# The last two experts' rows reach their frames through TensorE, and the work behind a mixture of experts is put in another order (two-layer encoder step, one core)

## What is computed

```python
def hier_moe(x, w_group, b_group, w_expert, b_expert, w1, w3, w2):
    xt = x.reshape(B * T, D)
    g_logits = xt @ w_group + b_group                 # 4 groups
    grp = argmax(g_logits);  p_grp = softmax(g_logits)[grp]
    e_logits = (xt @ w_expert + b_expert).reshape(-1, 4, 8)
    topv, topi = top_k(e_logits[grp], 2)              # 2 of the group's 8 experts
    gates = one_hot(grp) * (one_hot(topi) * softmax(topv)) * p_grp     # (T, 32)
    h = silu(xt @ w1[e]) * (xt @ w3[e]) * gates[e]    # per expert, width 256
    return sum_e(h @ w2[e])

for layer in (0, 1):
    h = h + mixer(rmsnorm(h, norm_mix[layer]))        # layer 1: short convolution
    h = h + hier_moe(rmsnorm(h, norm_ffn[layer]), ...)
```

## Time and profile before

| | |
|---|---|
| median of 3 runs | 1164.1 us |
| the profiled execution | 1163.0 us, span 1161.3 us |
| TensorE busy | 1012.0 us (87%) |
| VectorE, ScalarE, GpSimd busy | 390.5, 307.0, 189.6 us |
| mean granted TensorE clock | 0.941 |
| bytes moved | 282.80 MB, mean 244 GB/s |
| mixture of layer 0 / of layer 1, router to last scatter | about 360 to 637 / 870 to 1139 us |

### The profile page before, as it was taken

The page is one execution under the profiler, slowest core; times in us unless marked ns, Lnnn a source line. Parts: engine busy times, 40 slices in busy tenths (PEclk is TensorE's granted clock), DMA queues, the critical chain, the costliest instruction groups (busy, mean ns, idle before and its releaser), DMA issues.

```text
span 1161.3 us, 20224 instructions
## 1 busy us (share of the span) xinstructions
PE 1012.0 (87%) x8611; PEld 788.6 (68%) x8611; DVE 390.5 (34%) x861; ACT 307.0 (26%) x714; POOL 189.6 (16%) x188
## 2 busy tenths in 40 slices
PE   6999999989999899777875499999998999778781
PEld 6999898965898655444442399999996655444440
DVE  5242464257337211101101755546355111011104
ACT  6255344256224121101102421221131121011110
POOL 7344213120000223112111000000001222121110
PEclk9999998989899999989888699999999999898896
DMA  6432121420736999999996724243667999999976
GB/s 224 96 98 91 38 75 60 112 93 2 249 158 239 361 416 415 417 416 416 416 410 191 214 56 109 55 109 145 183 163 291 396 415 418 416 417 416 416 287 241
DMA packets 115011, 282.80 MB, mean 244 GB/s; under 512 B 23102, under 2 KB 70250, under 8 KB 98504
## 3 DMA queue, kind: packets, MB, share of 16 engines
q1 hardware_dynamic: 105192, 263.64, 61.1%
q0 software_dynamic: 9728, 17.85, 4.1%
HBM read 270.55 MB, written 27.02 MB: 256 GB/s over the span
## 4 chain that ended last, share of the span: by engine, by line
PE 62%; SPq 15%; DMA 15%; DVE 5%; issue 2%; ACT 1%; POOL 0%; DVEq 0%; POOLq 0%; ACTq 0%
PE banks L1046 12%; DMA w<-in_w_dram 11%; SPq L397 10%; PE banks L913 10%; PE banks L681 10%; PE banks L974 9%; PE banks L680 6%; SPq L400 5%; PE banks L985 4%; DVE H L1790 1%; PE banks L652 1%; DMA yab<-y_rows 1%; PE banks L874 1%; PE banks L858 1%; PE banks L968 1%
## 5 line engine op out<-in xcount | busy, mean ns | idle before, releaser
L974 PE MATMUL banks<-w,xgT 128*64 128x256 f32 x2048 | 261.5, 416 | 65.7 <-DMA w<-in_w_dram 64.5
L974 PEld LDWEIGHTS banks<-w,xgT 128*64 128x64 f32 x2048 | 161.9, 150 | 172.9 <-DMA w<-in_w_dram 72.9
L1728 DVE TENSOR_TENSOR hh<-banks,sg 128x128 f32<-128x128 f32 x64 | 18.6, 291 | 407.1 <-ACT sg L1294 407.1
L590 POOL DMA_INDIRECT y_rows<-ys,yidx x64 | 63.6, 994 | 381.4 <-ACT ys L1302 380.0
L985 PE MATMUL banks<-w,hT 128*64 128x512 f32 x512 | 116.9, 599 | 0.0
L1046 PE MATMUL banks<-xc_hi,wc_hi 128*128 128x272 f32 x384 | 111.0, 289 | 2.1 <-DVE xc_lo L1368 2.1
L1046 PE MATMUL banks<-xc_hi,wc_lo 128*128 128x272 f32 x384 | 111.2, 289 | 0.0
L1046 PE MATMUL banks<-xc_lo,wc_hi 128*128 128x272 f32 x384 | 110.6, 288 | 0.0
L586 POOL DMA_INDIRECT xr<-x_rows,gidx x32 | 33.5, 1046 | 400.0 <-DVE yidx L1714 382.2
L576 POOL TENSOR_TENSOR wab_lo<-wab,wab_hi 128x512 fp32r<-128x512 f32 x56 | 77.0, 1406 | 129.6 <-ACT wab_hi L1106 128.7
L681 PE MATMUL banks<-wab_hi,xc_hi 128*128 128x256 f32 (+1 forms) x320 | 93.7, 293 | 4.0 <-DVE xp_lo L1368 2.2
(11 more groups left out here) (283 smaller groups left out, 1765.1 us busy)
## 6 DMA issues: line engine op xcount, KB each, us to landing
w<-in_w_dram SPq DMA_DIRECT2D x192, 1024.0 KB, 23.0
wab<-in_w_in_ab_dram SPq DMA_DIRECT2D x13, 1024.0 KB, 5.2
wc<-in_w_in_c_dram SPq DMA_DIRECT2D x24, 512.0 KB, 5.3
yab<-y_rows SPq DMA_DIRECT2D x16, 512.0 KB, 6.7
wo<-in_w_out_ab_dram SPq DMA_DIRECT2D x4, 1024.0 KB, 7.1
x_rows<-XF SPq DMA_DIRECT2D x8, 512.0 KB, 3.3
wo<-in_w_out_c_dram SPq DMA_DIRECT2D x4, 1024.0 KB, 5.5
H<-in_x_prompt_dram SPq DMA_DIRECT2D x4, 512.0 KB, 8.9
```

The source lines that it names most:

```text
L590: pool.indirect_dma_start(y_dram[l][:, :], bass.IndirectOffsetOnAxis(ap=index.bitcast(U32), axis=0), ys[i][:, :], None, bounds_check=4 * T ...
L974: last = pe.matmul(bank[hb][64 * f:64 * f + 64, 0:2 * P].rearrange("p (w j) -> p w j", w=2), xgT[i][:, k, 64 * ab:64 * ab + 64], w13[s][:, ...
```

## The change

Seven edits, all in the mixtures and at their end.

1. **Experts 30 and 31** are no longer scattered. GpSimd scatters rows of zeros in their place at the start of the mixture (`zs_out`), so that `y_rows` is whole without them. SyncE's return loads wait for 30 experts instead of 32, and for these zero rows.
2. VectorE works out place and share of each frame in the last pair (8 small operations in `route`, 10 of 128 x 128 for `toks`), TensorE transposes them (`last_pair_T`, 10 transpositions behind the first pair's `hidden`), ScalarE copies them out (3 copies, `tkT_ok`, for which the first `rows_out` waits).
3. **`last_pair_rows`**: for each chunk 4 matmuls (weights `toks_T`, 64 rows; moving `ys`, 512 columns) give the last pair's share of 1024 features in two banks, and `combine` is now one more addition from PSUM. The two old operations are called `returned`.
4. **Router**: the two streams of 8 matmuls are taken by turns, after all chunks are there; one signal instead of two.
5. **Order at the boundary**: VectorE splits conv block 0 (`wc_lo`) only behind chunk 3; TensorE begins the first half with the two terms that don't need it; ScalarE makes `wc_hi` of block 0 between the squares of chunks 1 and 2.
6. `yab` lies at other addresses (free during the experts). SyncE's loads for the next router wait for the last `last_pair_rows` (`cb_mm`), since `toks_T` lies there.
7. The last mixture combines chunks in the order 0, 1, 2, 4, 3. Three semaphores of the recurrence are merged into `exp_ok`.

```diff
+COMBINE_BANKS = [0, 2, 4, 2, 6]
...
-        yab = [at(f"yab{c}", (132, 140, MISC, MISC + 8, MISC + 16)[c], [P, 2, D]) for c in range(NC)]
+        yab = [at(f"yab{c}", (132, 152, 160, 144, 172)[c], [P, 2, D]) for c in range(NC)]
...
+        SCATTERS = [NE // 4 - (j >= 2) for j in range(4)]
...
-                sp.wait_ge(y_mm, NE * (l + 1))
+                sp.wait_ge(y_mm, NE * l + NE - 2)
                 sp.wait_ge(cnt_ok, l + 1)
                 for j in range(4):
-                    sp.wait_ge(scat[j], 16 * (NE // 4) * (l + 1))
+                    sp.wait_ge(scat[j], 16 * SCATTERS[j] * (l + 1))
+                sp.wait_ge(zs_out, 32 * (l + 1))
...
             sp.wait_ge(lg_mm, 2)
+            sp.wait_ge(cb_mm, NC)
             router_load(1)
...
                 for u_ in range(2):
                     fetch(u_, gidx[:, u_:u_ + 1], xr_in[u_])
+                tie(pool.memset(ys[3][:], 0.0))
+                pool.wait_ge(ix_ok, 2 * l + 2)
+                for e in (NE - 2, NE - 1):
+                    pool.indirect_dma_start(y_dram[l][:, :], ... ys[3][:, :] ...).then_inc(zs_out, 16)
...
-                    for e in (2 * u_, 2 * u_ + 1):
+                    for e in (2 * u_, 2 * u_ + 1)[0:2 * (u_ < PAIRS - 1)]:
...
-                for p0, t, chunks, done in ((0, slice(0, 2 * P), 2, lgh_mm), (64, slice(2 * P, T), NC, lg_mm)):
-                    pe.wait_ge(xt_a, NC * (2 * l + 1) + chunks)
-                    pe.wait_ge(xt_d, NC * (2 * l + 1) + chunks)
-                    for k in range(KT):
+                pe.wait_ge(xt_a, NC * (2 * l + 2))
+                pe.wait_ge(xt_d, NC * (2 * l + 2))
+                for k in range(KT):
+                    for p0, t in ((0, slice(0, 2 * P)), (64, slice(2 * P, T))):
                         last = pe.matmul(bank[0][p0:p0 + NR, 0:t.stop - t.start], wr[:, k, :], XT[l][:, k, t], ...)
...
+                    if u_ == 0:
+                        last_pair_T()
...
+                        if e == 0:
+                            pe.wait_ge(tkT_ok, l + 1)
                         rows_out(SLOTS[l][e % 6], ab, y_mm)
...
+            def last_pair_rows(l, c):
+                b = COMBINE_BANKS[c]
+                for ab in range(2):
+                    for n in range(2):
+                        half = slice(64 * n, 64 * n + 64)
+                        w = toks_T[c // 2][half, c % 2, ab, :] if c < 4 else toks_T4[half, ab, :]
+                        last = pe.matmul(bank[b + n][0:ROWS[c], :], w, ys[2 + ab][half, :], start=ab == 0, stop=ab == 1)
+                last.then_inc(cb_mm, 1)
             mixture(0)
+            for c in range(3):
+                last_pair_rows(0, c)
...
-            for c in range(3):
-                norm_transpose(2, c)
+            norm_transpose(2, 0)
+            norm_transpose(2, 1)
+            pe.wait_ge(h_ok, NC + 2)
+            last_pair_rows(0, 3)
+            norm_transpose(2, 2)
+            frames_ready(1)
+            last_pair_rows(0, 4)
+            pe.wait_ge(wc_hi_ok, 1)
+            frames_ready(3)
+            conv_terms(0, 0, 0, (0, 1))
+            conv_terms(0, 0, 1, (0, 1))
+            pe.wait_ge(h_ok, NC + 4)
+            conv_terms(0, 0, 2, (0, 1))
             pe.wait_ge(wc_lo_ok, 1)
-            frames_ready(3)
-            for a in range(3):
-                if a == 2:
-                    norm_transpose(2, 3)
-                    norm_transpose(2, 4)
-                conv_terms(0, 0, a)
+            for a in range(2):
+                conv_terms(0, 0, a, (2,))
+            norm_transpose(2, 3)
+            norm_transpose(2, 4)
+            conv_terms(0, 0, 2, (2,))
             frames_ready(NC)
...
+            square(2, 0)
+            square(2, 1)
             conv_hi(0)
+            square(2, 2)
+            mixer_in_hi(2, range(3))
             conv_hi(1)
-            for c in range(3):
-                square(2, c)
-            mixer_in_hi(2, range(3))
...
+                    returned(0, 0)
+                    returned(0, 1)
+                    combine(0, 0)
+                    returned(0, 2)
+                    combine(0, 1)
+                    norm(2, 0)
+                    combine(0, 2)
+                    norm(2, 1)
+                    norm(2, 2)
+                    mixer_in_lo(2, xc_lo, range(3))
+                    returned(0, 3)
+                    combine(0, 3)
                     conv_lo(0)
...
+                    returned(0, 4)
+                    combine(0, 4)
+                    norm(2, 3)
+                    norm(2, 4)
+                    mixer_in_lo(2, xc_lo, (3, 4))
...
+            def combine(l, c):
+                n, b = ROWS[c], COMBINE_BANKS[c]
+                done = c if l == 0 else (0, 1, 2, 4, 3)[c]
+                dve.wait_ge(cb_mm, NC * l + done + 1)
+                h = H[0:n, c, :].rearrange("p (a d) -> p a d", a=2)
+                tie(dve.tensor_tensor(h, banks[0:n, b:b + 2, :], h, ALU.add))
                 dve.nop().then_inc(h_ok, 1)
```

More of the change, by code:

```diff
@@ L516, in _ @@
             mixture(1)
[L517 to L518 removed]
+            for i, c in enumerate((0, 1, 2, 4, 3)):
+                sp.wait_ge(h_ok, 3 * NC + i + 1)
                 dst = y_prompt[0, c * P:(c + 1) * P, :] if c < 4 else y_sample[0, :, :]
@@ L1077, in _ @@
             mixture(1)
+            for c in range(3):
+                last_pair_rows(1, c)
+            pe.wait_ge(h_ok, 3 * NC + 1)
+            last_pair_rows(1, 4)
+            pe.wait_ge(h_ok, 3 * NC + 2)
+            last_pair_rows(1, 3)
         @block.scalar
@@ L1723, in mixture @@
                 xg_high(0).then_inc(xg_d, 1)
+                for c in range(NC):
+                    n = ROWS[c]
+                    for e in range(2):
+                        last = dve.tensor_scalar(toks[c][0:n, e, :], slot_no[0:n, :], place[0:n, c, e:e + 1], share[0:n, c, e:e + 1],
+                                                 ALU.is_equal, ALU.mult)
+                last.then_inc(rk_ok, 1)
                 for u_ in range(PAIRS):
```

96 lines of the change are left out of this document (62 added, 34 removed).

## The result

| | before | after |
|---|---|---|
| median | 1163.18 us (8 runs) | 1166.95 us (8 runs, 1165.43 to 1168.04) |
| ratio | | 1.0028, 95% interval 1.0015 to 1.0041 |
| profiled execution, span | 1163.0, 1161.3 us | 1168.04, 1166.3 us |
| TensorE, VectorE, ScalarE busy | 1012.0, 390.5, 307.0 us | 1029.6, 411.2, 308.9 us |
| mean granted clock | 0.941 | 0.947 |

The forecast was 1164.2, in 1157.2 to 1170.8. The ratio is the one on record, with its interval; the quotient of the two medians alone is 1.0032. The profiled execution of after was the longest of its eight, 1.1 us above the median; its span is 5.0 us longer than that of before.

A forecast was written before the change was run, and what follows sets the result against it. The prediction took weight streaming to bound the mixtures and a chain of waits the rest. Terms of -1.7, -0.7, +6.0 and -3.5 us sum to +0.1, giving 1163.1, plus 1.1 for the median: 1164.2 us, range 1157.2 to 1170.8.

The forecast's parts named there:

- What bounds the kernel: Whole kernel: weight streaming at 416 GB/s sets the mixtures; outside them the chain of waits, including layer 0's long convolution piece.
- Router, -2.3 a layer: Router in both layers: matmuls taking turns need 3.9 us instead of 6.64, less 0.45 of waiting, so 2.3 us earlier.
- First pair, +0.6 and +1.6: First expert pair: added transpositions and copies delay the first `rows_out` 1.6 us; layer 0 gives back 0.6, layer 1 1.6.
- Return in layer 0, +6.0: Boundary after layer 0's mixture: rows come 4.6 us earlier, but VectorE's added work makes the second half 6.0 us later.
- chunk 3's matmuls ahead of chunk 2's transposition, I take 1.0: Layer 0's boundary, TensorE's order: chunk 2's low part comes about 1.0 us later than those of chunks 0 and 1.
- TensorE has done the first half by then: Layer 0's boundary: TensorE has finished the first half before the second can start, so nothing of the +6.0 comes back.
- Chunk 2's transposition at the full clock: Layer 0's boundary: transpositions count as work restoring the clock; otherwise chunk 2's eight take 2 us, not 1.
- Return in layer 1, -3.5: End of layer 1: loads start at 1130.3, VectorE ends 4.35 us earlier, the larger last output costs 0.9; net -3.5 us.
- behind expert 31 by 1143: End of layer 1: the last pair's matmuls for chunks 0 to 2 are behind expert 31 by 1143 us.
- B: Rival, chance 0.22: boundary costs only 3.2 us, router gives 2.8 twice, the end gives 4.4; 1157.3 us.
- C: Rival, chance 0.17: TensorE holds the boundary, 64-row halves one behind the other, 6.6 us a chunk; +9.5 there, 1170.7 us.
- D: Rival, chance 0.11: layer 1's return comes no earlier, the end gives nothing; 1167.7 us.

The follow-up runs named there:

- e1: The kernel before with only the router edit (16 matmuls by turns, one signal); 1159.61 us, ratio 0.9962 to before.
- e10: The changed kernel with TensorE's transposition of chunk 2 ahead of the last pair's matmuls for chunk 3; 1166.10 us, ratio 1.0013 to before.
- e3: The changed kernel with 14 idle matmuls in TensorE's gap ahead of chunk 3's transposition at the boundary; 1166.99 us, ratio 1.0008 to before.
- e11: The changed kernel with returned rows loaded before conv weights, chunk 2's transposition earlier, idle matmuls at boundary and first pairs, VectorE reordered; 1154.37 us, ratio 0.9923 to before.

## Why the prediction held, point by point

The time held within its range, but that says less than it seems: the forecast was a change of +0.1 us, the ratio says +3.3. The profiled spans differ by 5.0 (after's was its slowest run), and their terms are: the mixtures, router and first pair together, -1.1 and -1.4 (forecast -1.7 and -0.7; 260.68 us instead of 262.20 and 255.5 instead of 257.3 from the router's start to the marks used above, the router starting 0.46 later), the boundary +9.5 (+6.0), the end -2.6 (-3.5). So the terms missed in both directions, but most of the miss is the boundary's.

- **What bounds the kernel:** right. The router's saving (e1) and the delay of the long piece carry over in full.
- **Router, -2.3 a layer:** right. 4.08 us against 6.70, and 0.46 later: 2.2. e1 gave 4.4 for two (interval 2.6 to 6.3).
- **First pair, +0.6 and +1.6:** right in place and size (0.6 to 0.9, and 2.0). Missed: the clock, which makes it up to 3.5 in layer 1 when it falls there.
- **Return in layer 0, +6.0:** the mechanism was right, the size was not: from the conv weights' issue to the end of the long piece it is 195.4 us instead of 185.9, **+9.5**. By its steps: an addition 1.22 us (1.21 predicted), `wc_lo` 3.36, the wait ahead of the third norm 1.23 (1.8). The term "chunk 3's matmuls ahead of chunk 2's transposition, I take 1.0" was 2.7 us of VectorE's waiting, though the matmuls themselves took 3.79 us (4.2 forecast). And the step that said TensorE has done the first half by then, so nothing comes back, was read for time alone. Behind its idle time the clock fell: 2.5 us, in no case of mine. These two are 4.2 us more than forecast; less the 0.6 by which the third norm's wait came out shorter, that is 3.6, against the 3.5 that were missing. The first rows came 16.7 us behind the conv weights' issue, 16.3 forecast; but the 1.2 us "for completion" in that term stands in no row, so how its parts split is not shown.
- **Chunk 2's transposition at the full clock:** it took 1.40 us, between 1.09 and 1.97. The rule on transpositions is not settled: in e10 the clock was 0.50 through three of them until matmuls came at 656.55, which speaks for the rule of the Trainium skill that the prediction names. In the kernel before two stood back to back (654.64 to 658.31), and the clock was 1.00 at 660, ahead of any product; but in e1, with the same order, it was 0.50 until 662.
- **Return in layer 1, -3.5:** 2.6 by the trace. VectorE began 10.6 us earlier against expert 31's `hidden` (9.6 forecast), but took 21.3 us, not 19.2: 1.41 went on the first addition, which waited for the last pair's matmuls behind expert 31's own `hidden`, 5.31 us (3.67 before) with the clock at 0.50 at its start. I had those matmuls "behind expert 31 by 1143", 16.2 us behind the start of that `hidden` for three chunks; they began 12.1 us behind it, and the first addition started at 14.2, where without the wait it would have at 12.8.
- **Rivals.** B falls: the boundary was dear. C falls: chunk 3's four matmuls (8 records) took 3.79 us at a clock of 0.50, under the 5 us from which it decides and under the 6.6 of two halves one behind the other, so the 64-row halves run side by side. D falls: the loads came 12 us earlier against expert 31's `hidden`. Of my signs, the second half at "about 676.5" (679.63) and VectorE "without a gap but one" (a second one of 2.68 us) failed. No case of mine held that the order of the loads was worth more than all the rest: I had worked out that only 4.6 us of 7.2 would be won behind the conv weights, and took that as given.

Left open: in how many of the timed runs the clock fell at the pair or the boundary, since only one execution of each kernel has a profile. The mean granted clock of each run gives a hint. After's eight runs all have 0.947 or 0.948. E3's three shortest (1160.99 to 1163.66) have 0.951 to 0.955, its other eight 0.947 to 0.949, so filling one gap does not hold the clock everywhere in every run.

## What to carry to other kernels

When a change makes data ready earlier, look at what stands ahead of it in the same DMA queue and move that too; here this was worth 10.7 us, in a kernel that the change as a whole had made 3.3 slower. Work added to an engine that carries a stretch counts in full, so find it a gap first. A gap on TensorE can cost twice, once as time and once as clock behind it. Idle matmuls in it can hold the clock (e3), but they must end before the next work is there, or they become part of the chain (e11); so read their length from a trace.

## What the hardware showed that I had not expected

- Behind 3.10 us without work the mean granted clock was 0.85 and 0.81 in the two windows of 10 us, 2.5 us lost until the end of the long piece. Behind 1.84 us (e10) it stayed at 1.00. At the first pair gaps of 1.7 to 2.0 us were followed by 0.50 in some profiles and by 1.00 in others, where the code at the pair is the same.
- VectorE adds 1024 columns from PSUM to SBUF in 1.22 us, no more than the 1.28 us of its operation on the returned rows for the same width from SBUF alone. Its group in after:

```profile
L1890 DVE TENSOR_TENSOR H<-banks,H 128x1024 f32<-128x1024 f32 x8 | 9.8, 1224 | 1.7 <-PE banks L1076 1.4
```

- Fourteen idle fp32 matmuls of 128 columns (28 records) took 3.29 us at the boundary of e3, twice the 1.6 us that I had expected.
